# Hybrid decoder step: the last expert block's result goes to its tokens by products in the array, the overflow pass stands ahead of it, and the last gathered pair is turned one block earlier

## The reference, cut to what matters

```python
def hier_moe(x2d, ...):
    ...
    eid = grp[:, None] * EXPERTS_PER_GROUP + top_i          # two experts for each token
    combine = jnp.sum(jax.nn.one_hot(eid, N_EXPERTS) * weights[..., None], axis=1)
    for e in range(N_EXPERTS):
        h = jax.nn.silu(x2d @ moe_w_gate[e]) * (x2d @ moe_w_up[e])
        y = y + combine[:, e:e + 1] * (h @ moe_w_down[e])
    return y
...
xp = xp + f[:n_prompt_tokens]; xs = xs + f[n_prompt_tokens:]
y_prompt = rms_norm(xp, norm_final_w); y_sample = rms_norm(xs, norm_final_w)
```

## Time and profile before

| | us |
|---|---|
| median of three runs | 1101.46 (1100.73 to 1102.41) |
| the profiled execution | 1102.08 |
| its span in the trace | 1100.4 |
| PE / DVE / ACT / POOL busy | 1023.7 / 563.2 / 370.9 / 442.3 |

### The profile page before, as it was taken

How to read it: one execution, slowest core, us unless ns; L and a number is a source line. 1 busy time by engine, 2 the same in 40 slices (tenths; PEclk the granted TensorE clock), 3 DMA queues, 4 the chain that set the end, 5 groups by cost and what they waited for, 6 DMA issues and landing times. The chain is left out here.

```text
span 1100.4 us, 24864 instructions
## 1 busy us (share of the span) xinstructions
PE 1023.7 (93%) x10457; PEld 770.0 (70%) x10457; DVE 563.2 (51%) x1194; ACT 370.9 (34%) x796; POOL 442.3 (40%) x459
## 2 busy tenths in 40 slices
PE   5999999799999999999999999999997999997885
PEld 5777777588888887888888788884564555554442
DVE  6577787656565553777655446423264322221225
ACT  3444545545555443444344461000111111110113
POOL 7646646244565424877663335520001222221110
PEclk9999999999999999999999999999988999998998
DMA  8022221020000007541143114315958999999985
GB/s 260 12 76 72 81 82 39 9 77 4 4 5 4 4 4 182 173 115 40 39 145 112 49 66 173 120 52 219 421 226 312 404 415 413 416 417 416 410 353 233
DMA packets 86008, 182.99 MB, mean 166 GB/s; under 512 B 9897, under 2 KB 59589, under 8 KB 78218
## 3 DMA queue, kind: packets, MB, share of 16 engines
q1 hardware_dynamic: 79325, 168.59, 41.9%
q0 software_dynamic: 5088, 8.43, 2.1%
q10 hardware_dynamic: 1485, 4.39, 1.0%
HBM read 172.98 MB, written 17.55 MB: 173 GB/s over the span
## 5 line engine op out<-in xcount | busy, mean ns | idle before, releaser
L2321 POOL DMA_INDIRECT d_y<-tl_xn,ex_sidx x32 | 32.0, 1000 | 119.0 <-DVE tl_xn L2902 112.5
L2898 DVE SCALAR_TENSOR_TENSOR ex_sg<-tl_psA,ex_slot_rs,ex_sg 128x128 f32<-128x128 f32 x32 | 11.2, 351 | 124.4 <-ACT ex_sg L2673 124.2
L2316 POOL DMA_INDIRECT tl_xn<-d_tok,ex_gidx x16 | 16.8, 1051 | 139.5 <-DVEq L2893 80.8
L264 PE MATMUL psv<-xT,w_sum 128*128 128x260 f32 x256 | 61.5, 383 | 0.8 <-DVE uv_gu L1597 0.6
L226 POOL TENSOR_TENSOR w_sum<-w 128x512 f32<-128x512 f32 x16 | 21.2, 1325 | 94.1 <-PE mg_w L264 93.9
L264 PEld LDWEIGHTS psv<-xT,w_sum 128*128 128x128 f32 x256 | 48.5, 190 | 9.0 <-issue 1.0
L2673 ACT ACTIVATE ex_sg<-tl_psA,ex_slot_rs 128x128 f32<-128x128 f32 x32 | 11.7, 367 | 126.7 <-PE tl_psA L2514 126.7
L1060 PE MATMUL ck_b<-ck_X,ck_V 64*64 64x64 f32 x1280 | 49.4, 222 | 2.2 <-issue 1.1
L264 PE MATMUL rk_ps<-xT,rk_w 128*128 128x260 f32 x208 | 50.1, 384 | 0.0
L264 PE MATMUL rk_ps<-xS,rk_w 128*128 128x260 f32 x200 | 48.6, 386 | 0.0
L1060 PEld LDWEIGHTS ck_b<-ck_X,ck_V 64*64 64x64 f32 x1280 | 42.7, 134 | 3.9 <-issue 3.7
(11 more groups left out here) (645 smaller groups left out, 2812.0 us busy)
## 6 DMA issues: line engine op xcount, KB each, us to landing
wd<-in_moe_w_down SPq DMA_DIRECT2D x13, 1024.0 KB, 23.9
rk_w<-in_w_in SPq DMA_DIRECT2D x12, 1024.0 KB, 5.3
w_uv<-in_w_in SPq DMA_DIRECT2D x16, 512.0 KB, 5.2
w<-in_w_in SPq DMA_DIRECT2D x8, 1024.0 KB, 5.9
tl_x<-in_moe_w_down SPq DMA_DIRECT2D x8, 1024.0 KB, 19.8
xT<-in_moe_w_gate SPq DMA_DIRECT2D x5, 1024.0 KB, 17.4
xT<-in_moe_w_up SPq DMA_DIRECT2D x5, 1024.0 KB, 19.5
w<-in_proj_a SPq DMA_DIRECT2D x4, 1024.0 KB, 4.8
```

The source lines that it names most:

```text
L264: ins = eng.matmul(bank[:, 0:TH], w[:, k, :], x[:, k, :], start=(first and k == 0), stop=(last and k == NK // 2 - 1), skip_group_check=True)
L2316: eng.indirect_dma_start(out=xg[:, p % 2, :], out_offset=None, in_=m.d_tok, in_offset=bass.IndirectOffsetOnAxis(ap=gidx[:, p:p + 1], axis= ...
L2321: eng.indirect_dma_start(out=m.d_y2, out_offset=bass.IndirectOffsetOnAxis(ap=rows, axis=0), in_=yo[:, x, :], in_offset=None, bounds_check= ...
L2898: eng.scalar_tensor_tensor(out=sg[:, out, :], in0=psg[out][:, P:2 * P], scalar=scale, in1=sg[:, out, :], op0=ALU.mult, op1=ALU.mult).then_ ...
```

## The change

Block 31's result no longer goes to `d_y2`. Instead DVE builds, at block 8, a matrix `share` of each token's weight at its slot of expert 31 (`shares`, new); PE transposes it at block 9, ACT copies it back; and after block 31 `last_block` (new) multiplies it with block 31's result and adds that to the token rows: into `psA`, `psB` and `psT` for tiles 0, 1 and 2, and into `psB` and `psC` for the sample rows and tile 3, from where DVE adds it (`add_last`, new). POOL writes zeros to block 31's rows of `d_y2` (L2357, L2359 of the changed kernel), so that the loads of `fy` find zeros there. The overflow loop stands between block 30 and block 31 on every engine. Pair 16 is turned in block 29 (before: block 30). Of tile 1, DVE adds the first result itself (`lead`, new) and PE only the second. The `fy` tiles are loaded in the order 0, 1, 3, 2. `shares` is seven operations on DVE, its transposes five on PE.

```diff
 def turned_at(k):
-    return 0 if k % 2 else k // 2 + 1
+    return NE // 2 if k == NE - 3 else 0 if k % 2 or k == NE - 2 else k // 2 + 1
...
 @code.sync
-            for k in range(SLOTS, NE):
+            for k in range(SLOTS, NE - 1):
+                load_block(k)
             n = passes(eng)
             with eng.Fori(0, n) as q:
...
+            load_block(NE - 1)
...
             eng.wait_ge(s_y[0], n * 16 + NE // 2 * 16)
-            eng.wait_ge(s_y[1], NE // 2 * 16)
+            eng.wait_ge(s_y[1], (NE // 2 - 1) * 16)
+            eng.wait_ge(s_blanked, 16)
...
-            for j in range(NT):
+            for j in (0, 1, 3, 2):
                 eng.dma_start(fy[j // 2][:, j % 2, :, :], rows[j * P:(j + 1) * P]).then_inc(s_fy[j], 16)
...
 @code.gpsimd
+            eng.wait_ge(s_t, NE // 2)
+            eng.memset(xg[:, 1, 0:D // 2], 0.0).then_inc(s_blank, 1)
+            eng.wait_ge(s_blank, 1)
+            eng.indirect_dma_start(out=m.d_y2, out_offset=bass.IndirectOffsetOnAxis(ap=sidx[:, NE - 1:NE], axis=0),
+                                   in_=xg[:, 1, 0:D // 2], in_offset=None, bounds_check=4 * PITCH - 1, oob_is_err=False)\
+               .then_inc(s_blanked, 16)
...
+            scatter_block(NE - 5)
+            eng.wait_ge(s_t, NE // 2 + 1)
+            gather_now()
+            for k in range(NE - 4, NE - 1):
+                scatter_block(k)
...
 @code.tensor
+                if k == 9:
+                    eng.wait_ge(s_share, 1)
+                    for i in range(NTT):
+                        last = eng.transpose(psT[:, i // 4, (i % 4) * P:(i % 4 + 1) * P], share_t[:, i, :], m.ident[:, :])
+                    last.then_inc(s_share_t, 1)
...
+            def last_block(ps2, j, alone=False):
+                n = size[j]
+                for h, rows in enumerate(halves_of):
+                    last = eng.matmul(ps2[0:n, h, :], share_t[rows, at[j], 0:n], yo[rows, 1, :], start=alone, stop=alone,
+                                      skip_group_check=True)
+                return last
...
+            kept(psT, 2)
+            eng.wait_ge(s_list_x, 1)
+            eng.wait_ge(s_yo, n + NE)
             kept(psA, 0)
+            last_block(psB, NT, True).then_inc(s_last, 1)
+            last_block(psA, 0)
+            last_block(psC, 3, True).then_inc(s_last, 1)
+            combined(psA, 0)
+            eng.wait_ge(s_last_in, 1)
+            eng.wait_ge(s_led, 1)
             kept(psB, 1)
+            last_block(psB, 1)
+            combined(psB, 1, (1,))
+            last_block(psT, 2)
             combined(psT, 2)
...
 @code.vector
+            def add_last(j, nth):
+                dst = fx[:, j, :] if j < NT else fxs
+                eng.wait_ge(s_last, nth)
+                do(eng.tensor_tensor(by_half(dst), (psB, psC)[j < NT][0:size[j], :, :], by_half(dst), ALU.add))
+
+            def lead(j):
+                eng.wait_ge(s_fy[j], 16)
+                eng.scalar_tensor_tensor(out=fx[:, j, :], in0=fy[j // 2][:, j % 2, 0, :], scalar=m.weight[:, 0, at[j]:at[j] + 1],
+                                         in1=fx[:, j, :], op0=ALU.mult, op1=ALU.add).then_inc(s_led, 1)
...
             eng.wait_ge(s_fx, 16 * (NT + 1))
+            add_last(NT, 1)
+            eng.sem_inc(s_last_in, 1)
             sum_up(NT)
+            lead(1)
...
             scaled(1)
+            add_last(3, 2)
             sum_up(3)
```

More of the change, by code:

```diff
@@ L2190, in phase_tail @@
         at_slot_x = to_slot.rearrange("p (c t s) -> p c t s", c=2, s=CAP)
+        share = to_slot.rearrange("p (t x s) -> p t x s", x=2, s=CAP)
+        share_t = to_slot.rearrange("p (t s) -> p t s", s=P)
         work = to_x.rearrange("p (c t e) -> p c t e", c=2, e=NE)
@@ L2335, in _ @@
             eng.wait_ge(s_list, 2)
-            for p in range(1, NE // 2 + 1):
+            for p in range(1, NE // 2):
                 for k in range(max(0, 2 * p - 5), 2 * p - 3):
@@ L2345, in _, with gather_now @@
                     n = passes(eng)
[L2346 to L2351, removed]
+            eng.wait_ge(s_t, NE // 2)
[4 more added lines that the diff above has]
+               .then_inc(s_blanked, 16)
+            def gather_now():
                 eng.indirect_dma_start(out=xg[:, 0, :], out_offset=None, in_=m.d_tok,
@@ L2542, in _ @@
             eng.wait_ge(s_te2, NT)
-            for k in range(NE):
+            for k in range(NE - 1):
                 eng.wait_ge(s_xgT, 2 * ((k + 1) // 2) + 2)
@@ L2589, in kept, with combined @@
                                skip_group_check=True)
-            def combined(ps2, j):
+            def combined(ps2, j, choices=(0, 1)):
                 eng.wait_ge(s_fy[j], 16)
-                for c in range(2):
+                for c in choices:
                     for h in range(2):
@@ L2688, in _ @@
                 hidden(k % 2)
+                if k == 9:
+                    eng.wait_ge(s_share_t, 1)
+                    for b, to in enumerate((to_slot[:, 0:4 * P], to_slot[:, 4 * P:5 * P])):
+                        eng.activation(to, psT[:, b, 0:to.shape[-1]], ACT.Copy).then_inc(s_shared, 1)
                 if k == NE // 2:
@@ L2700, in _ @@
                 rows(0)
+            eng.wait_ge(s_gu, n + NE)
+            silu(1, slot_rs[:, NE - 1:NE])
+            eng.wait_ge(s_ht, n + NE)
+            hidden(1)
             flat = lambda ps2: ps2.rearrange("p h c -> p (h c)")
@@ L2966, in extra_indices, with shares @@
                 do(eng.tensor_scalar(last_pair, last_pair, -1 - PITCH, None, ALU.bitwise_and))
+                do(eng.tensor_copy(gidx_now[CAP:P, :], xidx[CAP:P, 1:2]))
                 eng.tensor_copy(gidx[CAP:P, NE // 2:NE // 2 + 1], xidx[CAP:P, 0:1]).then_inc(s_list_x, 1)
+            def shares():
+                mine_now = oh[:, :, :, NE - 1]
+                full = [P, NTT, CAP]
+                do(eng.scalar_tensor_tensor(out=lates[:, :, :], in0=rk[:, :, :], scalar=1.0, in1=mine_now, op0=ALU.add, op1=ALU.mult))
+                do(eng.tensor_tensor(low[:, :, :], m.weight[:, :, 0:NTT], mine_now, ALU.mult))
+                do(eng.tensor_tensor(lates[:, 0, :], lates[:, 0, :], lates[:, 1, :], ALU.add))
+                do(eng.tensor_tensor(low[:, 0, :], low[:, 0, :], low[:, 1, :], ALU.add))
+                for x in range(2):
+                    step.did(eng.scalar_tensor_tensor(out=share[:, :, x, :], in0=slots.unsqueeze(1).to_broadcast(full), scalar=1.0,
+                                                      in1=lates[:, 0, :].unsqueeze(2).to_broadcast(full),
+                                                      op0=ALU.add, op1=ALU.is_equal))
+                step.wait()
+                do(eng.tensor_tensor(share_t, share_t, low[:, 0, :].unsqueeze(2).to_broadcast([P, NTT, P]), ALU.mult))
+                eng.sem_inc(s_share, 1)
             def diagonals():
@@ L2991, in _ @@
                     extra_indices()
+                if k == 8:
+                    shares()
                 if k == NE // 2:
```

79 lines of the change are left out of this document (49 added, 30 removed).

## The result

| | before | after |
|---|---|---|
| median, compared side by side (20 runs each) | 1102.06 (1096.82 to 1106.23) | 1104.56 (1102.06 to 1110.14) |
| ratio after/before | | 1.003, 95% interval 1.0015 to 1.0044 |
| the profiled execution / its span | 1102.08 / 1100.4 | 1105.96 / 1103.5 |

The change makes the kernel 0.3% slower, about 3.3 us. The prediction was 1101.3 us (1099.0 to 1104.0), no change; the time lies above its range.

The account below looks back on a forecast made before the run. The weight stream was taken to set the pace to about 1065, then a chain of waits ending in DVE's list. There 1.46 us gained less 1.27 gave 0.2 us off the median 1101.46: 1101.3, range 1099.0 to 1104.0.

Parts of the forecast that it names:

- The stretch of the blocks: Blocks 8 to 10 and later: added DVE, PE, ACT and POOL work hidden by the weight stream; nothing taken.
- Overflow ahead of block 31: PE finishes the overflow block at 1060.4 to 1062; block 31's down ends at 1068.05 to 1069.2.
- Products: PE after block 31: fx rows land at 1069.3, two kept take 1.8 us each, last_block 0.9, ending at 1073.8.
- C: Rival, slower: PE falls to the lower clock at kept, costing 1.8 us, at most 4.5; 1103.1 to 1105.8; chance 0.09.
- X: Time the sample rows' share is in PSUM, where DVE's list begins: 1073.8, bounds 1072.5 to 1075.4.
- The way of the results: Overflow's scatter issued at 1062.9, lands at 1069.2, 3.1 us earlier; the second tile's results land at 1077.65.
- DVE's list: Sample sum ends at 1077.7, scaled(1) starts 1.46 us earlier, add_last(3) adds 1.27; last scaling ends 0.2 us earlier.
- Rival A: Faster: the new DVE operations vanish in idle time and the end comes 4.2 us earlier, 1097.3; chance 0.16.

Follow-up runs that it names:

- e8_zeros5: Changed kernel with block 31's rows written four more times during blocks 20 to 28; ratio 1.0048 against the kernel before.
- e7_best: Changed kernel with sample rows loaded first, tiles 2 and 0 on their own semaphore, last_block ahead of kept, DVE reordered; ratio 0.9987 against the kernel before.
- e11_best: Second run of the kernel of e7_best, with all remedies on the changed kernel; ratio 1.0000 against the kernel before.
- e1_split: Changed kernel with the sample rows' load first and PE's first kept waiting only for tiles 2 and 0; ratio 1.0015 against the kernel before.
- e2_busy: Changed kernel with 16 useless transposes on PE ahead of its wait for the rows; ratio 1.0014 against the kernel before.
- e12_memory: Changed kernel's block order, but block 31's result scattered through memory, without zeros, last_block, add_last or lead; second run, ratio 1.0001 against the kernel before.
- e3_first: Changed kernel with the sample rows' and tile 3's last_block products ahead of both kept on PE; ratio 1.0025 against the kernel before.
- both memory kernels: Two runs of the changed block order with block 31's result scattered through memory, without the new products or zeros; ratios 1.0006 and 1.0001 against the kernel before.

## Why the prediction was wrong, point by point

**The stretch of the blocks: right in the end, wrong in its cover.** I held PE's transposes at block 9 to be hidden by the weight stream. They were not: the copies of blocks 8 and 9, before and after, stand 6.75 and 7.30 us apart.

```profile
904.23 0.69 DVE L2902 COPY tl_xn<-psv 128x512 f32<-128x512 f32 x1 [0.97 <-PE psv L2524]
910.98 0.69 DVE L2902 COPY tl_xn<-psv 128x512 f32<-128x512 f32 x1 [1.19 <-PE psv L2524]
```

```profile
904.54 0.69 DVE L2964 COPY tl_xn<-psv 128x512 f32<-128x512 f32 x1 [0.97 <-PE psv L2547]
911.84 0.69 DVE L2964 COPY tl_xn<-psv 128x512 f32<-128x512 f32 x1 [1.19 <-issue]
```

The delay of 0.55 us stays to block 20 and is gone by block 22 (101.12 us behind block 6 before, 101.08 after), where PE waits for weights. Both PE and the DMA engines are full at 900; PE has no gap there, which the busy time of 5.00 in 5 us said. The zeros, which I held to cost nothing in place of block 31's scatter, cost 0.29 us in the stream (e8_zeros5).

**Overflow ahead of block 31: right.** Block 30's gate_up took 3.67 us without a wait, the last weights came at 1063.1, block 31's down ended at 1068.63 (forecast 1068.05 to 1069.2).

**Products: the step that failed.** The term "I take the middle, 1069.3" put the landing of the rows 1.77 us too early: kept started at 1071.07. I counted 15 us, the middle of 13.4 to 16.6, from the issue of the last tile at 1054.3. In after that tile was issued at 1054.95, and the set that `s_fx` counts was complete 16.1 us behind that. My sum named four loads and PE's wait counts five, but the fifth, the sample rows issued at 1056.07, is not what made it late: in e7_best and e11_best it is issued first and the last tile no earlier or later than in after, and DVE's wait for it and for tiles 1 and 3 still ends 178.98 and 178.94 us behind block 6's copy, where kept starts 178.87 behind it in after. What PE needed first, tiles 2 and 0, e1_split had there before 176.33. The upper bound of 1070.9 was sound, and the landing lay at it: in the trace of the kernel before, the last step of this semaphore stands at 1070.81, hidden by PE's turn, which ended at 1070.94. The change took that cover away. last_block itself went as forecast, 0.96 us apart against 0.9, its two half-height products side by side.

**The clock: a rival that came.** C had 0.09 and a price of 1.8 us; e2_busy and the trace measure 1.7. I judged it apart from the landing, with a gap of about 1 us; the late landing made the gap 2.44 us. These were one case, not two independent ones, and as one case they gave 1073.8 + 1.8 + 1.8 = 1077.4 for X. Either alone would have left the time inside the range, at most 1101.3 + 1.8 = 1103.1; both together give 1101.3 + 1.8 + 1.7 = 1104.8. The rule that I cited from the Trainium skill, TensorE: Matmul & The Clock Gate, section "What's actually happening", and set aside (the throttled clock is the default and activity releases it) agrees with after's row at 0.50. e8_zeros5 and e12_memory, as idle there and at full clock, do not bear out my reading of it, that a thin stretch alone brings the lower clock.

**The way of the results: right, in part by luck.** The overflow's scatter was issued at 1063.9, 1.0 us later than forecast, because block 30's landed that much later; it took at most 5.7 us instead of 6.3 and had landed by 1069.6 (forecast 1069.2). The second tile's results came at 1077.87 in e3_first, as its lead shows, 186.04 us behind block 6's copy (forecast 1077.65, 185.75 behind it).

**DVE's list: right.** From X to the end of the sample sum 4.02 us (forecast 3.9), from there to the first scaling 6.49 (6.9), add_last(3) 1.27 (1.27). Rival A did not occur, but the traces of e7_best and e11_best show what a part of it needed: another order on DVE and PE, not less work. Because the list is in order and begins at X, 3.36 of X's 3.65 us came through to the last scaling (1097.65 against 1094.3); the rest came back ahead of the first scaling.

**What stays open.** By their ratios e1_split, e3_first, e7_best and e11_best lie 1.9, 3.0, 1.6 and 3.1 us worse than their tails say; half an interval is 1.8 to 2.0 us, so e3_first and e11_best are outside it. A part is outside the span: the time is 1.72 us longer than the span on average in the kernel before and in both memory kernels, 1.94 to 2.30 in the kernels with products. What that is, and how often the clock falls in runs without a trace, was not tried.

## What to carry to other kernels

A semaphore that counts a set of loads makes each user wait for the last one: when work in front of such a wait is moved away, take the landing of the whole set at its late end, issue first what is needed first, and give it its own semaphore. Put the products that need no load into the gap; it keeps the clock up as well. Two late things that share a cause are one case with the sum of their prices.

## What was not expected of the hardware

- The length of PE's idle time alone did not decide on its clock. Ahead of kept, waits of 2.44 (after), 2.47, 2.70, 2.75 and 2.90 us were followed by the lower clock, waits of 2.46 (e12_memory) and 2.52 (e8_zeros5) were not; ahead of the first tile's sum, waits of 1.90 to 2.13 us were followed by it three times of three, while 1.82 and 2.00 us ahead of the turn were not the earlier trace rows. PE of e8_zeros5:

```profile
1069.94 1.98 PE L2635 MATMUL tl_psT<-w_lo,ident 128*128 128x512 f32 x4 [2.52 <-DMA wd<-d_x]
```

- The set of five loads was complete at the same time whichever was issued last: 178.87 us behind block 6's copy in after (the 32 KB of the sample rows last, 15.0 us behind its issue), 178.98 and 178.94 in e7_best and e11_best (a 512 KB tile last, 16.2 us behind its issue).
- A scatter of 0.12 MB (the queue of the indirect transfers moved 8.92 MB in e8_zeros5 and 8.43 in after, for four more of them) cost the weight stream 0.29 us.
